# Compression weights loaded first in their lane, and a new order of tiles in the last projection group of a hybrid decoder step

## The reference, cut to what matters

```python
xn = rmsnorm(x, W['ln_mix'])
p = xn @ W['w_in']                       # 1024 x 2908, columns cut into q_a, kv_a, q_idx, ...
q_a = rmsnorm(parts['q_a'].reshape(bsz, t, KVA, GA, DH), W['g_qa'])     # per head, DH = 64
kv_a = norm_k(parts['kv_a'].reshape(bsz, t, KVA, 2, DH), W['g_ka'])     # keys normed, values not
q_m = rmsnorm(parts['q_m'].reshape(bsz, t, HM, DHM), W['g_qm'])         # DHM = 128
...
# compress: blocks of rows through w_cmp1 (2 x 32 x 64 x 64), gelu(h + pe_h), w_cmp2
pe_h = jnp.einsum('crd,crdh->ch', W['cmp_pe'], W['w_cmp1'])
```

## Time and profile before

| | us |
|---|---|
| median of 3 runs | 2480.06 |
| lowest, highest | 2473.49, 2483.3 |
| the profiled execution | 2465.84 |
| its span | 2464.0 |
| PE busy | 1812.5 (74%) |
| DVE busy | 1736.5 (70%) |
| mean granted clock of PE | 0.815 |

### The profile page before, as it was taken

How to read it: one execution, slowest core, us unless ns; L and a number is a source line. 1 busy time by engine, 2 the same in 40 slices (tenths; PEclk the granted TensorE clock), 3 DMA queues, 4 the chain that set the end, 5 groups by cost and what they waited for, 6 DMA issues and landing times.

```text
span 2464.0 us, 25252 instructions
## 1 busy us (share of the span) xinstructions
PE 1812.5 (74%) x6723; PEld 1000.0 (41%) x6723; DVE 1736.5 (70%) x3924; ACT 705.7 (29%) x2093; POOL 827.6 (34%) x830
## 2 busy tenths in 40 slices
PE   5999889989889787975776676487674373974445
PEld 2457476664434333432222663354452232650121
DVE  2543567550369996679999779977567885786885
ACT  2000156650133442233333222123222121221222
POOL 0000023230023332243544532245236775332451
PEclk9899987999999898998999557798886565557766
DMA  4213050008369998699999989989999999989997
GB/s 132 52 57 124 29 200 1 1 19 341 120 265 379 394 410 341 257 367 360 411 401 419 353 337 399 379 332 402 348 371 386 337 394 416 360 336 423 393 369 309
DMA packets 171529, 722.40 MB, mean 293 GB/s; under 512 B 39705, under 2 KB 83122, under 8 KB 99386
## 3 DMA queue, kind: packets, MB, share of 16 engines
q0 software_dynamic: 84384, 577.16, 58.7%
q1 hardware_dynamic: 85282, 139.43, 15.6%
q10 hardware_dynamic: 1720, 4.19, 0.5%
HBM read 713.16 MB, written 11.61 MB: 294 GB/s over the span
## 4 chain that ended last, share of the span: by engine, by line
DVE 23%; DMA 16%; PE 13%; issue 11%; SPq 5%; POOL 3%; ACT 1%; DVEq 0%; ACTq 0%; POOLq 0%
DVE heads_t L3830 6%; DMA heads_t<-in_uv_tab,e_idx 4%; DMA ex_pairs<-in_uv_tab,e_idx 4%; SPq L1381 3%; PE ex_y_ps L3892 2%; DVE heads_t L3835 2%; DVE branch_rows_t L3835 2%; DVE ex_pairs L3835 2%; SPq L1380 2%; PE sl_at_l_ps L2046 2%; DMA is_ch<-in_cache_a_kidx,chunk_rows 2%; DMA branch_rows_t<-in_uv_tab,e_idx 1%; PE fq_acc L3553 1%; DMA fs_blocks<-in_w_branch 1%; DMA ex_early_pair<-in_uv_tab,e_idx 1%
## 5 line engine op out<-in xcount | busy, mean ns | idle before, releaser
L3858 ACT ACTIVATE ex_coef<-ex_dots 128x1 f32<-128x1 f32 x512 | 103.9, 203 | 1019.3 <-DVE ex_dots L3835 955.9
L3801 POOL DMA_INDIRECT ex_pairs<-in_uv_tab,e_idx x147 | 174.5, 1187 | 439.1 <-issue 174.5
L3801 POOL DMA_INDIRECT branch_rows_t<-in_uv_tab,e_idx x159 | 185.3, 1165 | 267.0 <-DVE heads_t L3830 185.5
L3801 POOL DMA_INDIRECT heads_t<-in_uv_tab,e_idx x146 | 170.3, 1166 | 237.7 <-DVE heads_t L3830 139.3
L3835 DVE CUSTOM_DVE_ANT_0 ex_pairs<-ex_pairs,heads_t 128x1024 f32<-128x1024 f32 x147 | 179.4, 1221 | 96.1 <-DMA ex_pairs<-in_uv_tab,e_idx 94.6
L3835 DVE CUSTOM_DVE_ANT_0 branch_rows_t<-branch_rows_t,heads_t 128x1024 f32<-128x1024 f32 x159 | 193.8, 1221 | 52.7 <-DMA branch_rows_t<-in_uv_tab,e_idx 50.6
L3835 DVE CUSTOM_DVE_ANT_0 heads_t<-heads_t 128x1024 f32<-128x1024 f32 x146 | 178.2, 1221 | 48.4 <-DMA heads_t<-in_uv_tab,e_idx 47.0
L879 PE MATMUL in_acc<-in_w,xn_t 128*128 128x512 f32 (+3 forms) x448 | 168.7, 532 | 2.0 <-ACT xn_t L423 0.8
L3892 PE MATMUL ex_y_ps<-ex_pairs,heads_t 128*128 128x512 f32 x212 | 113.0, 663 | 59.6 <-ACT heads_t L3865 53.0
L3860 ACT ACTIVATE ex_coef<-ex_coef,e_gate 128x1 f32<-128x1 f32 x512 | 150.8, 295 | 16.6
L3892 PE MATMUL ex_y_ps<-branch_rows_t,heads_t 128*128 128x512 f32 x224 | 121.2, 672 | 46.8 <-ACT heads_t L3865 40.0
(11 more groups left out here) (787 smaller groups left out, 3527.1 us busy)
## 6 DMA issues: line engine op xcount, KB each, us to landing
cs_ch<-in_cache_cmp_kv SPq DMA_DIRECT2D x256, 128.0 KB, 8.3
fq_wg<-in_w_gate SPq DMA_DIRECT2D x9, 2048.0 KB, 12.2
fq_wb<-in_w_branch SPq DMA_DIRECT2D x9, 1024.0 KB, 15.3
in_w<-in_w_in SPq DMA_DIRECT2D x4, 2048.0 KB, 10.8
fs_blocks<-in_w_branch SPq DMA_DIRECT2D x6, 1024.0 KB, 19.7
heads_t<-in_w_mem_kv SPq DMA_DIRECT2D x4, 1024.0 KB, 5.2
bias_t<-tmp_bias_back SPq DMA_DIRECT2D x4, 1024.0 KB, 9.7
ex_pairs<-in_w_gate SPq DMA_DIRECT2D x2, 2048.0 KB, 25.3
```

The lines of the kernel that those rows point to most:

```text
L3801: pool.indirect_dma_start(out=pair(s), out_offset=None, in_=i["uv_tab"], in_offset=bass.IndirectOffsetOnAxis(ap=idx[:, t, m:m + 1], axis=0 ...
L3858: act.activation(c, dots[:, t, m:m + 1], ACT.Gelu_apprx_tanh).then_inc(gelu_done, 1)
```

## The change

`load_compress_weights` becomes the first stage of the lane of tables, at step 4; the gains follow at step 10. In the last projection group the order of tiles is 0, STRIPS, 1, TP, 2, 3; the sums of tiles 0, 1, 2 and TP are rooted, inverted and applied before the copy of tile 3, and tile 3 is normed alone. `less_ident` is made at the beginning of the projection's stage.

```diff
         self.beside = tables
+        tables.next_step = 4
+        self.load_compress_weights()
         tables.next_step = 10
         self.gains()
         self.gains_ready = tables.before
-        self.load_compress_weights()
         tables.next_step = 13
         self.bias_tables()
...
-            widened = self.sem("in_widened")
+            widened, self.less_done = self.sem("in_widened"), self.sem("less_done")
...
-            units = [(j, t) for j in range(nj) for t in ((0, 1, 2, 3, STRIPS, TP) if j == 0 else (0, 1, 2, STRIPS, 3, TP))]
+            orders = [(0, 1, 2, 3, STRIPS, TP)] + [(0, 1, 2, STRIPS, 3, TP)] * (nj - 2) + [(0, STRIPS, 1, TP, 2, 3)]
+            units = [(j, t) for j in range(nj) for t in orders[j]]
...
+                    def root_part(count, part):
+                        act.wait_ge(sums_done, count)
+                        act.activation(part, part, ACT.Sqrt).then_inc(root_done, 1)
...
-                    root(nj - 1)
+                    root_part(nj, sums[nj - 1][:, :TP - 1])
+                    root_part(nj, sums[nj - 1][:, TP:])
+                    root_part(nj + 1, sums[nj - 1][:, TP - 1:TP])
...
-                        if t == TP:
+                        if t == TP and j < nj - 1 or j == nj - 1 and t in (TP - 2, TP - 1):
                             dve.sem_inc(sums_done, 1)
...
+                    dve.tensor_scalar(self.less[:], self.ident[:DB, :DB], -1.0, None, ALU.mult).then_inc(self.less_done, 1)
...
+                        if u == U - 1:
+                            break
...
-                    add_squares(nj - 1, TP)
-                    invert(nj - 1)
-                    for t in range(NT):
+                    add_squares(*units[U - 2])
+                    scale(nj - 2, TP)
+                    invert_part(nj, sums[nj - 1][:, :TP - 1])
+                    invert_part(nj + 1, sums[nj - 1][:, TP:])
+                    for t in (0, 1, 2, TP):
                         scale(nj - 1, t)
+                    dst, src = place(U - 1)
+                    dve.wait_ge(mm_done, U)
+                    dve.tensor_copy(dst, src).then_inc(odd_out, 1)
+                    add_squares(*units[U - 1])
+                    invert_part(nj + 2, sums[nj - 1][:, TP - 1:TP])
+                    scale(nj - 1, TP - 1)
...
-                    dve.tensor_scalar(less[:], ident8, -1.0, None, ALU.mult).then_inc(self.less_done, 1)
```

More of the change, by code:

```diff
@@ L920, in invert, with invert_part @@
                         c.link(dve.reciprocal(sums[j], sums[j]))
+                    def invert_part(count, part):
+                        dve.wait_ge(root_done, count)
+                        c.link(dve.reciprocal(part, part))
                     def scale(j, t):
@@ L951, in _ @@
                                 scale(j - 1, k)
-                    add_squares(nj - 1, TP)
-                    invert(nj - 1)
-                    for t in range(NT):
-                        scale(nj - 1, t)
+                    add_squares(*units[U - 2])
[3 more added lines that the diff above has]
+                    for t in (0, 1, 2, TP):
+                        scale(nj - 1, t)
+                    dst, src = place(U - 1)
[4 more added lines that the diff above has]
+                    scale(nj - 1, TP - 1)
     def keep_rows(self, pairs):
         pr, vals, w_idx, g_nsa = self.pr, self.vals, self.w_idx, self.g_nsa
-        less, ident8, self.less_done = self.less, self.ident[:DB, :DB], self.sem("less_done")
         s, gates_out = self.s, self.gates_out
```

## The result

| | before | changed |
|---|---|---|
| median, us (20 runs each) | 2469.41 | 2448.99 |
| lowest to highest | 2453.87 to 2485.51 | 2429.49 to 2467.05 |
| the profiled execution | 2465.84 | 2441.17 |
| its span | 2464.0 | 2439.4 |

The ratio is 0.9906 with a 95% interval of 0.9882 to 0.9930: on 2469.41 that is -23.2 us, between -29.1 and -17.3; the two medians themselves differ by 20.4. One run of the changed kernel, 2467.05, is in the slower state and is left out of the ratio. The forecast was -23.4. The median of before over 20 runs is 10.7 lower than that over the first three, from which the forecast started, so its own number, 2456.7, lies 7.7 above the median found. The median found, 2448.99, lies at the very edge of the forecast's own range (2449 to 2464) and inside the range with the rivals (2445 to 2471).

A forecast was written before the change was run, and what follows sets the result against it. PE's work plus its stalls was taken to bound the block; -14.3 - 4.0 - 2.3 - 2.8 = -23.4 us, put on the median 2480.06, gave 2456.7 us. Own range 2449 to 2464, with rivals 2445 to 2471.

The forecast's parts named there:

- the rivals: Only the head counts: 2464, chance 0.14; gains land late: 2471, 0.06; half clock elsewhere: 2493, 0.05; stretch falls away: 2447, 0.05.
- Term 1: Head of the program: with the compression weights loaded first, POOL's iota starts at 49.7 instead of 63.98; -14.3 us.
- Term 2: Last projection group: less DVE work behind PE's last matmul, projection ends at about 300.7 to 301.0, not 304.94; -4.0 us.
- term 3: Start of PE's turn: with `less_ident` made earlier, PE no longer waits for DVE's `keep_rows` instructions; -2.3 us.
- Term 4: PE's turn: it starts sooner after PE stops, so its first 12 and 28 instructions run at full clock; -2.8 us.
- What bounds the kernel: PE's list of work plus its stalls, notably 50 to 64 us, where engines wait for a stage whose weights they don't need.
- The price of the loads on SP: Eight DMAs ahead of group 1's weights take 10 us, at most twice that; hidden by the cover, so no cost.
- The rival of the late gains: Head: gains land so late behind the small packets that the wait stays at 49 us; 2471 us, chance 0.06.
- The root of group 5: Last group: ACT copies tile 1 and roots by 283.5; DVE inverted at 284.27 before, so the root is not late.
- The cover: Last group: DVE reaches the samples' copy at 289 to 290, PE's last tile needs it at about 291; 1 to 2 us.
- The gain passed through: Behind the block's closing barrier the remaining 2135 us are unchanged, so the whole gain reaches the kernel's end.

The follow-up runs named there:

- the head alone: The kernel before with only the compression weights' load moved to the first stage of its lane: first attention at 312.26 us, ratio 0.9973 (0.9939 to 1.0008).
- the root-early kernel: Changed kernel with the loads behind group 1's weights and the last group's root of group 5 behind tile 0's copy, not tile 1's: first attention at 308.58 us.
- the held loads: Changed kernel with the loads behind group 1's weights, issued only when the second tile's rows are transposed: ratio 0.9892 (0.9845 to 0.9940).

## Why the prediction was right, step by step

The profiled executions differ by 20.8 us at the first attention. By the forecast's terms:

| term | forecast | changed against before, one profile each | over the experiments |
|---|---|---|---|
| 1, head | -14.3 | -11.6 (iota 63.98 to 52.38) | -11.4 to -13.0 in three profiles of the change |
| between iota and PE's last matmul | 0 | -0.5 (233.96 to 233.42) | from the iota to the projection's end 232.1 to 243.9, by the clock and the stall |
| 2, last group | -4.0 | -4.2 (7.00 to 2.78 behind PE's last matmul) | PE idle 2.89 to 2.90 before the turn wherever both tail edits are in |
| 3, `less_ident` | -2.3 | -2.3 (2.41 to 0.11) | -2.3 alone; +2.3 when taken back |
| 4, clock in the turn | -2.8 | -2.1 (21.53 to 19.40) | -0.9 to -2.8 (20.6 to 18.7) |
| sum at the first attention | -23.4 | -20.8 | -20.3 to -22.0 in the three profiles |
| behind it | 0 | -3.8 | scatter: 28 us wide |

**What bounds the kernel** was read rightly: the stall at 50 us was a wait for a stage's end on every engine, and needed nothing of the weights. Putting the same stage ahead of the positional sum brought a stall back, also on DVE, which needed nothing of the weights there.

**The price of the loads on SP** was 10 us with a ceiling of 20: they took from 5.59 to 24.83, 19.2 us. Behind both 2 MB loads it was 22.2 and 22.3 (7.22 to 29.56), and held back until 18.0 it was 11.5 and 12.2, so the price grows with what stands ahead in the queue. The weights of group 1 were issued at 25.32 and landed 8.0 later, at 33.3, as forecast (32 to 33) and 21 us ahead of their use at 54.75. (Before, their issue began at 5.5 and not at the 6.1 that I had taken, so they landed at 21.8, and the move cost them 11.5 us.) The rival of the late gains did not come: nothing waited for them.

**Term 1 was mis-sized.** The step was "POOL's iota starts at 49.7": I let everything up to 49.57 stand as it was. I weighed what the small packets do to the loads behind them, and not what happens at the load ahead of them. All five profiles with the loads right behind the first 2 MB have this load landing after 12.3 to 12.8 us; of the eight others seven have it at 11.5 to 12.2 and one, with no small packets near it, at 12.4. In the two latest of the eight, 12.2 and 12.4, the inputs were late already: PE's very first transposes began at 13.35 and 13.41, and at 12.87 to 13.17 in the other six. So the order goes with a landing some 0.7 us later, and late inputs with nearly as much. The microsecond from 16 to 17 us, first in the trace before and then in that of the change (the last two numbers are the DMA share and GB/s):

```profile
16.00:17.00 1.00, 0.95 (x5) 0.68 (x4) 0.00 (x0) 0.97 (x4) 0.00 (x0) 1.00 1.04 406
...
16.00:17.00 1.00, 0.68 (x4) 0.28 (x2) 0.07 (x1) 0.97 (x4) 0.00 (x0) 1.00 1.31 209
```

In the five profiles with the small packets right behind the load the rate is 191 to 251 GB/s there, at a share of 1.31 to 1.33; in the eight others it is 399 to 414. So the small packets are being moved before the load ahead of them has landed (17.67 here). How they hold the landing up is not shown. In all thirteen the tile starts within 0.25 us of the landing. The other part of the loss is the tile's length. Its first weight loads take 0.34 us each in place of 0.19, as at half speed, although the granted clock of that stretch is recorded as 1.00:

```profile
18.77 0.34 PEld L881 LDWEIGHTS in_acc<-in_w,xn_t 128*128 128x128 f32 x1 [0.52 <-issue]
...
21.62 0.19 PEld L881 LDWEIGHTS in_acc<-in_w,xn_t 128*128 128x128 f32 x1 [0.24 <-issue]
```

That is the 8.72. PE's idle time ahead of the tile (1.10 us in the changed kernel) does not decide it: the head alone had the same idle time (1.09) and a tile of 7.11, and the root-early kernel had none of note and 8.19. What decides it, the traces do not show. On the mean of the five profiles the tile starts 0.8 us later than in the three with the loads behind the gains (17.50 against 16.72) and takes 1.2 longer (8.29 against 7.13); the two make up the 2.0 by which their mean iota (51.68) misses 49.7. What the held loads won at the head (iota at 50.0 to 50.4) was not there at the attention (307.8 to 308.1 against 306.8 to 308.6), which goes with the lower clock shown above. I count term 1 as -12 and not -14.

**Term 2 and term 3** were right to 0.2. The root of group 5, which I had called not late, kept DVE waiting for 2.43 us, and nothing came of it; a cast waited 0.54 us for the page table, which I had not seen. The cover I counted as 1 to 2 us was 1.09.

**Term 4** was right in sign and depends on luck in size. With the same 2.89 us of idle time PE's first 12 instructions took 1.53 to 2.82 and the next 28 1.75 to 3.26. At 5.21 us of idle time and above (four profiles) the first 12 took 2.79 to 2.82 each time. Taking the row at 298 to 302 for the new place of the turn was an argument from one execution; the mean from the turn to the attention over the three profiles of the change is 19.6, so -1.9.

**The gain passed through**: the ratio over 20 runs (-23.2) and the difference at the first attention (-20.8; -21.1 over three profiles) agree within the interval. The -3.8 behind it in the profiled pair is small against the 28 us by which that part scatters. That the total met the forecast within 1 us is in part luck: the edits themselves give about 21, as the two medians do (20.4), and the interval of 17.3 to 29.1 can't tell 21 from 23.4.

No kernel here is shown to beat the changed one: the held loads have 0.9892, whose interval holds 0.9906.

## What to carry to other kernels

Where several lanes share in-order engines, a stage that only POOL and SP work in still stops every engine that has reached the next stage of that lane. Put such a stage where no engine can reach its end before it is done, which here is the start of the program, and check with one kernel that puts it elsewhere. At the end of a group, count what is still to be normed after PE's last matmul, and bring all of it but one tile ahead of that matmul, even where a tile that needs no norming has to leave the last place for it. And price a moved transfer in both directions of its queue, for the loads behind it and for the one just ahead of it.

## What I had not expected of the hardware

- PE's granted clock fell also where PE was busy without a pause (0.50 from 80 to 90 us, PE busy for 10.00 of 10), and it differed between executions of nearly the same list: with the iota 2.6 us earlier the stretch behind it took 5.2 us longer (iota to projection's end 239.0 against 233.8).
- The same idle time of 2.89 us ahead of the turn was followed by full speed in some executions and by half speed in others (1.53 and 2.82 us for the same 12 transposes); the four with 5.21 to 9.41 us were all followed by half speed (2.79 to 2.82).
- Eight loads in 8,544 small packets took 10 us of SP's time in an empty queue, 19.2 us behind one load of 2 MB and 22.2 to 22.3 us behind two.
- With small packets right behind it in the queue, also the load just ahead of them landed later: 12.3 to 12.8 us after its issue, against 11.5 to 11.9 in the six profiles with other loads there and the inputs on time.
- The part behind the first attention, 2124 to 2152 us long for the same instructions, is longer where the mean granted clock of the run is lower: 0.812 to 0.814 in the three longest, 0.823 and 0.824 in the three shortest. The held kernel's first profile does not fit (2144.7 at 0.822).
